# Issuing the experts' down-weight loads from ScalarE's queue instead of SyncE's, in a mixture-of-experts layer

## The reference, cut to what matters

```
xt = rms_norm(x)                                   # 1024 tokens x 1024
top_s, top_idx = group_limited_top8(sigmoid(xt @ w_router))
for each expert e (64), for each block of its tokens:
    xb = xt[tok]                                   # gather rows
    hb = silu(xb @ w_e_gate[e]) * (xb @ w_e_up[e]) # 1024 -> 256 + 256
    yb = (hb @ w_e_down[e]) * g[:, None]           # 256 -> 1024
    acc = acc.at[tok].add(yb)                      # scatter with add
```

## Time and profile before

| | |
|---|---|
| median of 3 runs | 1825.13 us (1820.29 to 1825.42) |
| the profiled execution | 1824.83 us, span 1823.1 us |
| mean granted TensorE clock | 0.986 |
| PE busy | 1739.3 us, 95% of the span |
| DVE, ACT, POOL busy | 1304.6, 916.9, 785.9 us |
| DMA | 363.39 MB, 199 GB/s over the span |

### The profile page before, as it was taken

How to read it: one execution, slowest core, us unless ns; L and a number is a source line. 1 busy time by engine, 2 the same in 40 slices (tenths; PEclk the granted TensorE clock), 3 DMA queues, 4 the chain that set the end, 5 groups by cost and what they waited for, 6 DMA issues and landing times.

```text
span 1823.1 us, 32565 instructions
## 1 busy us (share of the span) xinstructions
PE 1739.3 (95%) x8044; PEld 1407.3 (77%) x8045; DVE 1304.6 (72%) x1485; ACT 916.9 (50%) x1104; POOL 785.9 (43%) x658
## 2 busy tenths in 40 slices
PE   7899999999999999889999999999999999999897
PEld 5788888888788777767777777787777877777786
DVE  7999999954265347858777877767777877677454
ACT  5100100035501123557767777776676767677665
POOL 3357668745466450045444444433433433344000
PEclk9999999999999999989999999999999999999999
DMA  4111112222333443499898999999889999997431
GB/s 155 52 46 46 46 46 80 92 93 93 110 138 112 136 150 111 145 323 367 283 295 273 337 307 305 319 274 344 271 269 310 314 288 312 290 279 228 149 116 70
DMA packets 118199, 363.39 MB, mean 199 GB/s; under 512 B 23696, under 2 KB 40208, under 8 KB 109968
## 3 DMA queue, kind: packets, MB, share of 16 engines
q1 hardware_dynamic: 70608, 276.58, 42.0%
q0 software_dynamic: 28608, 69.55, 15.6%
q10 hardware_dynamic: 18944, 16.78, 2.7%
HBM read 323.98 MB, written 76.85 MB: 220 GB/s over the span
## 4 chain that ended last, share of the span: by engine, by line
PE 75%; DMA 6%; issue 5%; DVE 3%; ACT 2%; POOLq 2%; POOL 1%; ACTq 1%; DVEq 0%
PE bank L123 10%; PE bank L125 10%; PE bank L124 10%; DMA xg<-h_rows,cur 6%; PE bank L1139 4%; PE bank L1145 4%; PE bank L1140 4%; PE bank L1120 4%; PE bank L1116 4%; PE bank L1115 4%; PE bank L1103 3%; PE bank L1104 3%; PE bank L1092 2%; PE bank L1221 2%; PE bank L1219 2%
## 5 line engine op out<-in xcount | busy, mean ns | idle before, releaser
L1872 DVE TENSOR_TENSOR gu_lo<-gu_raw,gu_hi 128x1024 fp32r<-128x1024 f32 x260 | 306.4, 1220 | 20.7 <-ACT gu_hi L1463 20.3
L123 PE MATMUL bank<-x_hi,w_hi 128*128 128x512 f32 x768 | 302.6, 394 | 7.6 <-ACTq L1289 6.2
L125 PE MATMUL bank<-x_hi,w_lo 128*128 128x512 f32 x768 | 299.9, 390 | 0.0
L124 PE MATMUL bank<-x_lo,w_hi 128*128 128x512 f32 x768 | 299.9, 390 | 0.0
L822 POOL DMA_INDIRECT acc_rows<-y,cur x98 | 165.3, 1686 | 306.6 <-ACT y L1459 290.6
L1608 DVE SCALAR_TENSOR_TENSOR bank<-a_buf,c_w_dw,bank 128x1024 f32<-128x1024 f32 x232 | 276.8, 1284 | 0.0
L1463 ACT CAST gu_hi<-gu_raw 128x1024 fp32r<-128x1024 f32 x260 | 259.8, 1049 | 0.0
L1115 PE MATMUL bank<-gu_hi,xh 128*128 128x512 f32 x512 | 206.4, 403 | 0.0
L1116 PE MATMUL bank<-gu_lo,xh 128*128 128x512 f32 x512 | 201.3, 393 | 0.0
L1120 PE MATMUL bank<-gu_hi,xl 128*128 128x512 f32 x512 | 195.4, 402 | 3.1 <-DVE gu_lo L1872 3.1
L814 POOL DMA_INDIRECT xg<-h_rows,cur x100 | 140.0, 1400 | 103.3 <-POOL cur L809 59.4
(11 more groups left out here) (313 smaller groups left out, 3260.8 us busy)
## 6 DMA issues: line engine op xcount, KB each, us to landing
gu_raw<-in_w_gu SPq DMA_DIRECT2D x256, 512.0 KB
dn_raw<-in_w_dn SPq DMA_DIRECT2D x64, 1024.0 KB
w_raw<-in_w_mix SPq DMA_DIRECT2D x60, 512.0 KB, 3.2
acc_t<-acc_rows SPq DMA_DIRECT2D x16, 512.0 KB, 4.8
first_x<-in_x SPq DMA_DIRECT2D x8, 512.0 KB, 7.8
ga_d<-stage ACTq DMA_DIRECT2D x8, 512.0 KB, 2.6
gb_d<-stage ACTq DMA_DIRECT2D x8, 512.0 KB, 2.6
gb_in<-gb_d SPq DMA_DIRECT2D x8, 512.0 KB, 3.6
```

The lines of the kernel that those rows point to most:

```text
L123: nc.tensor.matmul(o, wh[:, cols], x_hi[:, k, t], start=(i == 0), stop=False)
L124: nc.tensor.matmul(o, wh[:, cols], x_lo[:, k, t], start=False, stop=False)
L125: last = nc.tensor.matmul(o, wl[:, cols], x_hi[:, k, t], start=False, stop=(i == len(ks) - 1))
L1872: nc.vector.tensor_tensor(gl[s][:, w], rg[s][:, w], gh[s][:, w], ALU.subtract).then_inc(gu_split, 1)
```

## The change

The load of the down weights leaves SP's loop. ACT issues it instead, at the top of a step, ahead of `round_rows`: in step `e` for expert `e+1`, once expert `e-1`'s down weights, which were in the same buffer, have been split. In the second half of the loop's body this stands in a branch that is skipped in the last round. The up weights stay with SP.

```
-                        if p == 2:
-                            wait_at(sp, dn_split, r * 4 + (2 * s - 2), g)
-                            sp.dma_start(rd[1 - s][:], flat_row(i["w_dn"], r * 2 + (s - 1))).then_inc(dn_in[1 - s], 16)
                         wait_at(sp, gu_split, r * 8 + (4 * s - 7 + p), g)
                         sp.dma_start(rg[s][:, w], flat_row(i["w_gu"], e)[:, w]).then_inc(gu_in[s][p], 16)
-            sp.wait_ge(dn_split, 2 * (E - 1))
-            sp.dma_start(rd[1][:], i["w_dn"][E - 1]).then_inc(dn_in[1], 16)
...
+                    def load_down():
+                        wait_at(act, dn_split, e * 2 + 2, g)
+                        act.dma_start(rd[1 - s][:], flat_row(i["w_dn"], nc.s_assert_within(e + 1, 0, E - 1, skip_runtime_bounds_check_because=(
+                            "the last round is left out")))).then_inc(dn_in[1 - s], 16)
+
+                    if s:
+                        with act.If(r < E // 2 - 1):
+                            load_down()
+                    else:
+                        load_down()
                     round_rows(1 - s, b)
```

## The result

The changed kernel takes 1859.97 us in the median of 4 runs (1856.48 to 1864.7), the kernel before 1825.28 us. The ratio is 1.0208, with a 95% interval of 1.0188 to 1.0228. The profiled execution has a span of 1854.9 us, 31.8 us more than before.

What follows compares the result with a forecast made beforehand. PE, busy 860.6 of 900 us in the expert stage, was taken as the bound, with DMA share at 0.92. Terms 37.7 + 6 + 3 = 47 us on 1824.8 us gave 1872 us, range 1821 to 1903.

Steps and rivals of the forecast that it cites:

- a third loaded queue: Expert stage: down weights on ACT's queue take turns from POOL's gathers, up to 2.9 us each; 1872 us, chance 0.67.
- 13 waits, 2.9 us each, 37.7 us: PE's existing waits for the further block's gather each grow 2.9 us, 37.7 us in all; bounds 0 and twice that.
- 20 gathers in time today, 6 us: Further blocks' gathers now in time: those with under 2.9 us to spare become awaited by PE; 6 us, bounds 0 and 58.
- The clock, 3 us: PE's clock halves for 3.4 us behind waits, 1.7 us a dip; more dips cost 3 us, bounds 0 and 12.
- the signs that I named: Profile after: q10 some 66 MB more, `xg` waits 50 to 80 us and far more often, 10 us gathers, more half clock.
- the first rival: No change: third queue costs nothing, as SP's and ACT's queues are served as one or gathers hold themselves up; 1825, chance 0.13.
- SP's issues and the up weights: SP loses 63 issues and up weights no longer queue behind down weights; nobody waits for either, so gain 0.
- The moment of the load: Load's issue time: unchanged in short steps, 6 us later in long steps, shifting load into the steps behind them.
- ACT's issue: ACT gains 63 issues of 0.33 us, expected to pass under the `y` copy; value 0, bounds 0 and 21 us.
- Late down weights: Load lands in 10.5 us of 15 available, value 0; if late, ACT waits at L1467, about 1850, chance 0.03.
- Faster, since SP's queue runs dry: SP's queue, a third of its bytes gone, may be empty during the critical gather; 1789 at best, 1807 for half, chance 0.12.
- ACT is held: Issue delays ACT at `hth` and `y`, so POOL's scatter and gather go late and PE waits; 21 us, 1846, chance 0.05.

Runs made afterwards that it cites:

- act_early: Changed kernel with ACT issuing the down-weight load at the earlier moment, behind the first block's result copy, also in long steps: 1849.48 us, ratio 1.0159 to the kernel before.
- sp_late: Kernel before, down-weight loads still on SP but behind the up weights and held until ACT reaches the top of a step: 1821.82 us, ratio 1.0003.
- act_small: Kernel before plus one small load of 128 x 32 bytes from ACT's queue in each of 64 steps: 1823.49 us, ratio 0.9998.
- after_early_gather: Changed kernel with POOL issuing the further block's gather ahead of the first block's in a short step before a long one: 1805.83 us, ratio 0.9902.

## Why the prediction was right, and where its sizes were off

**Sign and mechanism: right, and shown.** The forecast was a third loaded queue, taking turns from POOL's, and PE waiting longer for the further block's gather. The queue alone gives most of the loss (act_early), a later moment on SP's queue and the issues give none (sp_late, act_small), and the loss all but goes when that gather is issued earlier (after_early_gather). Three queues alternate by packet as two did in the earlier trace rows.

**Size: 35 us measured where 47 were forecast.** Term by term:
- *13 waits, 2.9 us each, 37.7 us.* The waits grew by 20.1 us in all. The term was mis-sized: about 1.5 us each, not 2.9. I had priced the whole load on top of what the gather waited for already, as 15 packets per engine of 0.193 us, q1's mean. The rows show 8 packets per engine at 0.31 us, 2.5 us. More important, most of these packets were there before: 82 of 128 in the gather of the earlier trace rows, 6.6 of 8 per engine in the mean. What the third queue adds is above all the turns that q1's up weights take beside them; 8 turns of 0.14 us are 1.2 us by my estimate, and 1.2 us is what the weights' time in the two sets of rows differs by; the other 0.8 us there are q0's own packets. An incomplete coincidence is not the reason, since 7.9 of the 8 packets fall within the gathers after. The growth differs from block to block, 0.5, 1.9 and 3.2 us in the rows above; what sets it stays open.
- *20 gathers in time today, 6 us.* No more are awaited than before: 12 against 13. The term is about 0; only the wait for a first block's gather is new, 0.9 us.
- *The clock, 3 us.* It cost 10.6 us. I had reckoned with few dips more; there are ten against six, five of them twice as long, and in the kernel after each of the waits of 2.8 us and over has one. The fall can come within the wait, as the 1.08 us for the eight matmuls show.

The first two terms were too large by 18 and about 5 us, the third too small by 8. That the sum missed by no more than 12 us owes something to luck.

Of the signs that I named, q10 moves 66 MB more (82.84 against 16.78), gathers of over 10 us are on the chain, and there is more half clock. But PE's wait for `xg` stayed just under my 50 to 80 us, and came 12 times, not far more often than 13. I also took q0's packets of 0.32 us for the gather's. In the earlier trace rows they are those of 1244 to 1246 us, behind its landing at 1244.45; within it, in 1239 to 1241 us, q0's 107 packets take 0.480 x 32 / 107 = 0.14 us each:

```profile
q1 hardware_dynamic: 112, 0.45, 55.2%
q0 software_dynamic: 107, 0.39, 48.0%
```

The sum doesn't use the 0.32 us, but the first rival rests on it in part.

**The parts costed at nothing.** SP's issues and the up weights: right; PE's wait for `gu_lo` is 3.0 us, 3.1 before. The moment of the load: a later one costs nothing on SP's queue (sp_late), though with the third queue it may cost some 0.5%. ACT's issue: nothing on PE, but not for the reason that I gave. It does not pass under the `y` copy; `xh` waits for the sequencer by 43 us more in sum, and the slack at `xh` itself and at `hth` pays. Late down weights: ACT never waits at L1462 for them.

**The rivals.** "Faster, since SP's queue runs dry" did not come about; DMA is busy 0.90 of the stage, and the three queues' shares in 849 to 851 add up to 101%. "ACT is held" is refuted in the main by act_small; its small load does not wait for `dn_split`, but in the changed kernel too PE's waits are for gathers, not for ACT.

## What to carry to other kernels

A transfer moved to another issuing engine's queue is not free, even when its bytes and its time of issue stay the same: it opens one more queue that takes turns on the same 16 engines, and whoever is waited for in the other queues pays, by the time that the packets of the queues beside it take. Ask which transfer's landing the bound engine waits for, and keep the number of loaded queues, and the size of the packets in them, small beside it; here prefetched weights, which nobody awaited, were best left in one queue. The larger gain lay in issuing the awaited gather ahead of one that could wait.

## What the runs showed of the hardware that I had not expected

- A load with 8 KB rows goes in packets of 8 KB, 0.31 us each, and gets as many turns as a queue with 4 KB packets (65 to 63). Issuing it as two loads with 4 KB rows made the kernel before 0.4% faster (0.9962, 0.9947 to 0.9978) with the same bytes and one more issue per step.
- The Trainium skill (DMA: Bandwidth & Descriptors, section Rules for kernel authors) says that spreading transfers over SP, ACT and GpSimd "doesn't help" the bandwidth and only saves issue time. The rows agree on bandwidth, 291 GB/s over 790 to 1690 us against 296; but here the spreading was not neutral, it cost 2.1%.
- The TensorE clock fell to 0.51 for 3.4 us behind a wait of PE of 2.43 us; behind one of 2.78 us, at 1462.63 in the same trace, it did not fall. Longer waits cost clock on top of time: 10.6 us of PE's busy time beside 21.0 us of waits.
